# Second feed-forward part: six of eight weight pairs by seven products, three sum buffers, x added in the output, and low parts made two granules at a time

## The chip, the cores and the metric

The kernel runs on 1 core of one Trainium2 chip. The metric is the device time of one execution in microseconds (us), lower is better. Engines by their names in the profile: PE (TensorE, matrix products), DVE (VectorE), ACT (ScalarE), POOL (GpSimd) and SP (SyncE); the last two mainly start DMA transfers. Each engine runs its own instructions in the order written, and engines wait for each other by semaphores.

## What is computed

Two transformer-like blocks over 256 tokens of width 2048, all in fp32. The change lies in the last part of the second block, the feed-forward part with relu squared, called FFN 2 here:

```python
D_MODEL = 2048; SEQ = 256; D_FF_2 = 4 * D_MODEL
h2 = rms_norm(x, g_ff[l])
x = x + jnp.square(jax.nn.relu(h2 @ w_ff1[l])) @ w_ff2[l]
```

The first block has a feed-forward part of its own (FFN 1, gated by silu), which uses some of the same helper functions.

## The kernel before

**Numbers in two parts.** Each fp32 operand is split into a high part (fp32r, a copy by ACT) and a low part (the number minus its high part, by DVE). A product is three matmuls: high x high, low x high, high x low. Each matmul here has a stationary 128x128 and a moving 128x512 operand.

**Weights.** SP loads them by 1 MB into `raw`, a ring of four slots of two *granules* each; a granule is 2 chunks of 128 rows x 512 columns. ACT (`hi`) writes the high part into `w_hi`, DVE (`lo`) the low part into `w_lo`; both are rings of only 4 granules. `hi` of a granule waits in `gran_used` until PE has used the granule four before it; `lo` waits for `hi`; PE waits for both (`hi_ready`, `lo_ready`). The load into a raw slot waits for the `lo` of what was there.

**Turns.** FFN 2 handles 8192 hidden columns in turns of 1024 (`block2(at, i)`, i = 0 to 6). A turn has first 8 *units* 0 to 7: unit u is the pair of chunks 2u, 2u+1 of w_ff1 over 1024 columns (two granules). Then four *panels* 2 to 5 of w_ff2: 4 granules each (g = 0 to 3, written (panel, g)), 12 matmuls a granule, which multiply the hidden columns of the turn before and are 512 columns of the output each. The hidden columns made by turn i are thus used in turn i+1. The last turn has four more panels, 6 to 9.

**Units by seven products.** An *ordinary* unit is 8 block products, 24 matmuls. A unit *by products* takes 7 products (21 matmuls) as in Strassen's scheme in Winograd's form: it needs four sums of weight blocks (`sums_seven` on DVE: three instructions into `t_sum`), their high parts (`hi_sums`, ACT) and low parts (`lo_sums`, DVE: two instructions), the low parts of three blocks (`lo_blocks`, 128x1536) and four sums of token blocks, made once (`s_forms`, `first_forms`). Turn 0 has units 1, 3, 5, 7 by products (`SEVEN`), turns 1 to 6 units 0, 1, 3, 5, 7 (`FIVE`). There are two sum buffers. The sums of units 0 and 1 of the next turn are made while PE is in panel 5.

**Behind the units.** `recombine` (DVE) puts the products together into `hid` and `gates` (two rows of 512 columns). ACT takes relu times the token's factor (`relu_rows`) into another buffer, DVE multiplies the two (scalar_tensor_tensor), `flip` transposes in blocks (DVE), `move` on POOL finishes the transpose by 16 DMAs, and `hid_turn` makes the high part (ACT) and the low part (DVE) of the result, `low_hi` and `low_lo`, which panels 2 to 5 of the next turn read.

**Output.** PE accumulates a panel in one of two bank pairs in PSUM (q0 and q1, `pairs`), or `aux`. After panels 2 to 5 DVE adds it to x, which lies in SBUF (`xres`), by `add_x`, and counts `evac_done`; `bank_free` on PE waits for that before the pair's next use. At the end SP stores `xres` to the output.

**Order.** Each engine's order is written out by hand in its own `block2`. In DVE's, around panel 5: lo of panel 5 with `sums_seven(0)` in between, `lo_sums(0)`, `add_x(4)`, `sums_seven(1)`, `lo_blocks(0)`, `add_x(5)`, `lo_blocks(1)`, `lo_sums(1)`.

## Time and profile before

| | us |
|---|---|
| median of 3 runs (2574.84 to 2575.89) | 2574.9 |
| span of the profiled execution | 2573.7 |
| PE busy | 2567.3 (100%) |
| DVE busy | 2015.8 (78%) |
| ACT busy | 1451.4 (56%) |
| POOL busy | 536.5 (21%) |
| turn 0 of FFN 2 (1938.67 to 2023.08) | 84.41 |
| turn 2 of FFN 2 (2107.05 to 2191.02) | 83.97 |

The profiled execution is told by its span, from the first to the last instruction. Busy times of PE overlap between matmuls, since their ends are modelled, so the distance between two starts tells what a matmul takes. In the text *busy* says nothing of waits; what an engine waited for stands in square brackets behind a row of a timeline.

### The profile page before, as it was taken

How to read it: one execution, taken by the hardware profiler on the slowest of the kernel's cores; microseconds unless marked ns; L12 is line 12 of the kernel's file. 1: busy time of each engine (PE TensorE's matmuls, PEld its weight loads, DVE VectorE, ACT ScalarE, POOL GpSimd, SP SyncE). 2: the span in 40 equal slices, each digit the busy share in tenths (PEclk: the TensorE clock that was granted, in tenths of full speed). 3: DMA queues.
4: the chain of work that ended last, by engine and by line, in shares of the span. 5: the costliest groups of instructions: out<-in, count | busy, mean ns of one | idle time of the engine just before them, and what ended most of it. 6: DMA issues, size and time to landing. Idle time of an engine off the chain costs nothing.

```text
span 2573.7 us, 34186 instructions
## 1 busy us (share of the span) xinstructions
PE 2567.3 (100%) x11501; PEld 2134.4 (83%) x11501; DVE 2015.8 (78%) x2102; ACT 1451.4 (56%) x1615; POOL 536.5 (21%) x1034
## 2 busy tenths in 40 slices
...
GB/s 274 210 206 212 216 197 208 255 214 209 209 238 246 245 241 244 247 242 243 240 291 216 210 183 195 174 191 211 223 202 215 231 206 218 201 220 206 206 228 154
DMA packets 291153, 564.76 MB, mean 219 GB/s; under 512 B 28512, under 2 KB 41872, under 8 KB 290544
## 3 DMA queue, kind: packets, MB, share of 16 engines
...
q10 hardware_dynamic: 176, 0.07, 0.0%
...
## 4 chain that ended last, share of the span: by engine, by line
PE 97%; DVE 1%; DMA 1%; SPq 0%; DVEq 0%; ACT 0%; issue 0%; ACTq 0%
PE pair L2491 22%; PE pair L2486 22%; PE pair L2495 22%; PE pair L2776 8%; PE aux L2776 6%; PE aux L2761 3%; PE aux L2755 3%; PE aux L2758 3%; PE pair L2758 1%; PE pair L2755 1%; PE pair L2761 1%; PE aux L2653 0%; DMA raw<-in_w_ffn_down 0%; PE aux L2648 0%; PE pair L2573 0%; PE pair L2566 0%
## 5 line engine op out<-in xcount | busy, mean ns | idle before, releaser
L845 ACT ACTIVATE w_hi<-raw 128x1024 fp32r<-128x1024 f32 (+1 forms) x786 | 818.2, 1053 | 722.1 <-PE pair L2495 571.4
L1499 DVE TENSOR_TENSOR w_lo<-raw,w_hi 128x1024 fp32r<-128x1024 f32 (+1 forms) x788 | 937.7, 1214 | 342.1 <-ACT w_hi L845 323.2
L2486 PE MATMUL pair<-w_hi,lhs_hi 128*128 128x512 f32 x1568 | 422.6, 391 | 0.8 <-ACT lhs_hi L897 0.8
L2491 PE MATMUL pair<-w_hi,lhs_lo 128*128 128x512 f32 x1568 | 419.7, 389 | 0.6 <-DVE lhs_lo L1552 0.5
L2495 PE MATMUL pair<-w_lo,lhs_hi 128*128 128x512 f32 x1568 | 419.7, 389 | 0.0
L766 POOL DMA_DIRECT2D arena<-arena x528 | 262.4, 603 | 668.9 <-DVE arena L2003 291.0
L2491 PEld LDWEIGHTS pair<-w_hi,lhs_lo 128*128 128x128 f32 x1568 | 294.2, 188 | 63.0 <-DVE lhs_lo L1552 1.4
L2495 PEld LDWEIGHTS pair<-w_lo,lhs_hi 128*128 128x128 f32 x1568 | 294.0, 188 | 62.2 <-DVE w_lo L1499 1.0
L2486 PEld LDWEIGHTS pair<-w_hi,lhs_hi 128*128 128x128 f32 x1568 | 292.2, 188 | 60.6 <-ACT lhs_hi L897 1.2
L2486 PE MATMUL pair<-w_hi,low_hi 128*128 128x512 f32 (+1 forms) x992 | 263.4, 387 | 0.0
L2491 PE MATMUL pair<-w_hi,low_lo 128*128 128x512 f32 (+1 forms) x992 | 262.0, 386 | 0.0
L2495 PE MATMUL pair<-w_lo,low_hi 128*128 128x512 f32 (+1 forms) x992 | 261.7, 385 | 0.0
L2491 PEld LDWEIGHTS pair<-w_hi,low_lo 128*128 128x128 f32 x992 | 185.7, 188 | 36.3
L2495 PEld LDWEIGHTS pair<-w_lo,low_hi 128*128 128x128 f32 x992 | 185.5, 188 | 36.3
L2486 PEld LDWEIGHTS pair<-w_hi,low_hi 128*128 128x128 f32 x992 | 185.5, 188 | 36.0
L1180 ACT ACTIVATE w_hi<-raw 128x1536 fp32r<-128x1536 f32 x74 | 110.3, 1490 | 150.2 <-PE aux L2776 93.9
L777 POOL DMA_DIRECT2D arena<-arena x256 | 125.1, 497 | 251.9 <-DVE arena L1545 181.6
L2042 DVE TENSOR_TENSOR t_lo<-t_sum,t_hi 128x1024 fp32r<-128x1024 f32 x148 | 174.2, 1218 | 0.4 <-ACT t_hi L1189 0.2
L1189 ACT ACTIVATE t_hi<-t_sum 128x1024 fp32r<-128x1024 f32 x148 | 150.7, 1053 | 28.7 <-PE aux L2776 18.2
L2033 DVE TENSOR_TENSOR w_lo<-raw,w_hi 128x1536 fp32r<-128x1536 f32 x74 | 130.1, 1758 | 35.6 <-ACT w_hi L1180 21.0
L786 POOL DMA_DIRECT2D xres<-sums x36 | 46.8, 1314 | 437.8 <-ACT sums L1199 399.0
L2761 PE MATMUL aux<-w_lo,lhs_hi 128*128 128x512 f32 x372 | 124.6, 389 | 0.0
(366 smaller groups left out, 3244.1 us busy)
## 6 DMA issues: line engine op xcount, KB each, us to landing
raw<-in_w_ff SPq DMA_DIRECT2D x128, 1024.0 KB, 5.2
raw<-in_w_in SPq DMA_DIRECT2D x118, 1024.0 KB, 5.3
raw<-in_w_ffn_down SPq DMA_DIRECT2D x44, 1024.0 KB, 5.1
raw<-in_w_ffn_gate SPq DMA_DIRECT2D x80, 512.0 KB, 6.6
raw<-in_w_ffn_up SPq DMA_DIRECT2D x80, 512.0 KB, 7.5
raw<-in_w_out SPq DMA_DIRECT2D x32, 1024.0 KB, 5.7
...
xres<-sums POOLq DMA_DIRECT2D x36, 512.0 KB, 9.8
```

Source lines behind the costliest of these rows:

```text
L766: pool.dma_start(dst[f * 32:(f + 1) * 32, a], src[a * 32:(a + 1) * 32, f]).then_inc(moved, 16)
L777: pool.dma_start(turn_t[n % 2][f * 32:(f + 1) * 32, a], turn_x[n % 2][a * 32:(a + 1) * 32, f]).then_inc(row_moved[n % 2], 16)
L845: nc.scalar.activation(w_hi[:, at.slot(p, k), :, 0:width], raw[:, at.raw_slot(p, k), 2 * h:2 * h + 2, 0:width], ACT.Copy).then_inc(hi_read ...
L1189: nc.scalar.activation(t_high[:, 2 * h:2 * h + 2], t[:, 2 * h:2 * h + 2], ACT.Copy).then_inc(t_hi_ready, 1)
L1499: v.tensor_tensor(w_lo[:, at.slot(p, k), :, 0:n], raw[:, at.raw_slot(p, k), 2 * h:2 * h + 2, 0:n], w_hi[:, at.slot(p, k), :, 0:n].bitcast( ...
L2033: v.tensor_tensor(two_slots(w_lo, at, p, k)[:, 1:4], raw[:, at.raw_slot(p, k), 1:4], two_slots(w_hi, at, p, k)[:, 1:4].bitcast(F32), ALU.s ...
L2042: v.tensor_tensor(t_low[:, 2 * h:2 * h + 2], t[:, 2 * h:2 * h + 2], t_high[:, 2 * h:2 * h + 2].bitcast(F32), ALU.subtract).then_inc(t_lo_r ...
L2486: nc.tensor.matmul(ps[:, t, 0:n], hi_t[:, ch, tok], w_hi[:, s, c, 0:n], start=start and k == 0 and c == 0, stop=False)
L2491: nc.tensor.matmul(ps[:, t, 0:n], lo_t[:, ch, tok], w_hi[:, s, c, 0:n], start=False, stop=False)
L2495: mm = nc.tensor.matmul(ps[:, t, 0:n], hi_t[:, ch, tok], w_lo[:, s, c, 0:n], start=False, stop=stop and 2 * k + c == kch - 1)
L2761: mm = nc.tensor.matmul(bank[t, w], lhs_hi[:, ch, tok], w_lo[:, s, w, :], start=False, stop=u == 6 and c == 1 and (t, w) == (1, 0))
L2776: mm = nc.tensor.matmul(bank, s, t, start=fresh and first and a, stop=last and z)
```

## The change

- In turns 1 to 6 units 0, 1, 3, 4, 6, 7 go by products (`SIX`), in turn 0 units 1, 3, 4, 6, 7 (`FIVE`). Units 2 and 5 are ordinary.
- There are three sum buffers (`ring`). The third lies over `xres`, whose first three quarters are stored to the output before FFN 2 (SP, `x_stored`).
- Panels 2, 3 and 4 are no longer added to x on DVE: ACT copies them (`copy_part`) into `gates` or `hid`, and POOL adds them to the output by an accumulating DMA (`add_part`). Panel 5 is still added by `add_x`.
- Relu squared is made on ACT alone, in place (`relu_squares`: two Relu, one Square); DVE's multiplications go.
- `lo_two` makes the low parts of two granules in one instruction, 128x2048, and counts both when it is done.
- The orders of DVE, ACT, POOL and PE in a turn are rewritten. In `seven` the product with block B21 comes third, then the two with T1 and T3, then T2 (before: T2 third); this holds for FFN 1 too.

The diff, cut to its core:

```diff
-FIVE = (0, 1, 3, 5, 7)
+FIVE = (1, 3, 4, 6, 7)
+SIX = (0, 1, 3, 4, 6, 7)
+MAIN = {SEVEN: SEVEN, FIVE: FIVE[1:], SIX: FIVE[1:]}
...
+    ring = [(over_x(xres), [t_hi2[:], t_lo2[:, :, 2 * N:3 * N]], over_x(t_lo2)),
+            (halves(t_sum[0]), halves(t_hi), halves(t_lo[0])),
+            (halves(t_sum[1]), halves(t_hi1), halves(t_lo[1]))]
...
+            sp.wait_ge(evac_done, At("out2").panel(2) + 1 + EVAC_CREDIT)
+            sp.dma_start(token_rows(out[0])[:, :, 0:3 * N], xres[:, :, 0:3 * N]).then_inc(x_stored, 16)
...
+            def add_part(j, i):
+                pool.wait_ge(sums_copied, i * 3 + (COPIES1 + j + 1))
+                pool.sem_inc(moving, 1)
+                pool.dma_start(token_rows(out[0])[:, :, j * N:(j + 1) * N], hid if j == 1 else gates,
+                               accum_op=ALU.add).then_inc(parts_added[j % 2], 16)
+            move(NB1 + T_FF2)
+            pool.wait_ge(x_stored, 16)
+            with pool.Fori(0, TURNS2 - 1) as i:
+                for n in range(2):
+                    move(i * 2 + (NB1 + T_FF2 + 1 + n))
+                for j in range(3):
+                    add_part(j, i)
...
+            def relu_squares(rows):
                 for t in range(TOK):
-                    nc.scalar.activation(dst[:, t, :], src[t], ACT.Relu, scale=x_inv[:, t:t + 1])
+                    nc.scalar.activation(rows[:, t, :], rows[:, t, :], ACT.Relu, scale=x_inv[:, t:t + 1])
+                act.drain()
+                nc.scalar.activation(rows, rows, ACT.Square)
                 act.drain().then_inc(act_ready, 1)
-            def block2(at, i, last=False, five=True):
+            def copy_part(at, p, j, i):
+                panel_done(at, p)
+                if p < 4:
+                    act.wait_ge(flipped, i * 2 + (NB1 + T_FF2 + 3 + j))
+                if j == 2 or not isinstance(i, int) or i > 0:
+                    act.wait_ge(parts_added[j % 2], i * 16 if j == 1 else i * 32 + 8 * j)
+                nc.scalar.activation(hid if j == 1 else gates, pairs[at.pair(p)][:], ACT.Copy
+                                     ).then_inc(sums_copied, 1)
...
+            def block2(at, i, last=False, units=SIX):
                 n = i + TURNS1
                 b = i * 2 + NB1
...
+                act.wait_ge(gran_used, at.gran(0) + SPLIT)
+                if units == FIVE:
+                    hi_sums(3, n, units)
+                hid_turn(b, 0, T_FF2 - 1)
+                hi_ordinary(at, 2, None)
+                hi_seven(at, 3, None)
+                hi_sums(4, n, units)
+                hi_seven(at, 4, None)
+                hi_ordinary(at, 5, None)
+                hi_sums(6, n, units)
+                hi_seven(at, 6, None)
+                hi_sums(7, n, units)
+                hi_seven(at, 7, None)
                 hi(at, 2, 0, 2)
                 act.wait_ge(products, n * 3 + 1)
                 nc.scalar.activation(first_product, aux[:, 0, :], ACT.Copy).then_inc(product_copied, 1)
+                hid_turn(b + 1, 4, T_FF2 - 1)
                 hi(at, 2, 2, 4)
                 act.wait_ge(gates_ready, n + 1)
...
+                relu_squares(gates)
                 hi(at, 3, 0, 1)
...
+                relu_squares(hid)
                 hi(at, 3, 1, 4)
+                copy_part(at, 2, 0, i)
+                if units == FIVE:
+                    act.wait_ge(s_sums_ready, 4)
+                    nc.scalar.activation(zero_hi[:], zero_sum[:], ACT.Copy).then_inc(s_hi_ready, 1)
                 hi(at, 4, 0, 4)
...
+                copy_part(at, 3, 1, i)
                 hi(at, 5, 0, 4)
...
                 else:
                     nxt = At("ffn2", i + 1)
...
+                    hi_sums(0, n + 1, SIX)
+                    copy_part(at, 4, 2, i)
+                    hi_seven(nxt, 0, None)
+                    hi_sums(1, n + 1, SIX)
+                    hi_seven(nxt, 1, None)
+                    hi_sums(3, n + 1, SIX)
...
+            def lo_two(at, p, k):
+                dve.wait_ge(hi_ready, at.gran(p, k) + 2)
+                v.tensor_tensor(two_slots(w_lo, at, p, k), raw[:, at.raw_slot(p, k)],
+                                two_slots(w_hi, at, p, k).bitcast(F32), ALU.subtract).then_inc(lo_ready, 2)
...
+            def block2(at, i, last=False, units=SIX):
                 n = i + TURNS1
                 b = i * 2 + NB1
...
+                if units == FIVE:
+                    sums_seven(at, 3, n, units)
+                    lo_sums(3, n, units)
+                    dve.wait_ge(x_stored, 16)
                 hid_turn(b)
...
+                lo_two(at, *unit(2))
+                lo_blocks(at, 3)
+                sums_seven(at, 4, n, units)
+                lo_sums(4, n, units)
+                lo_blocks(at, 4)
+                lo_two(at, *unit(5))
+                sums_seven(at, 6, n, units)
+                sums_seven(at, 7, n, units)
+                lo_sums(6, n, units)
+                lo_blocks(at, 6)
+                lo_sums(7, n, units)
+                lo_blocks(at, 7)
+                lo_two(at, 2, 0)
+                if units == SIX:
+                    dve.wait_ge(parts_added[0], i * 32)
+                    dve.wait_ge(parts_added[1], i * 16)
+                recombine(at, n, 3, units, lambda: hid_turn(b + 1, 4))
+                lo_two(at, 2, 2)
                 dve.wait_ge(act_ready, b + 3)
...
+                flip(b + (2 + T_FF2), by_chunk(gates), n_split=1)
+                lo_two(at, 3, 0)
+                lo_two(at, 3, 2)
+                if units == FIVE:
+                    pair_forms(0, zero_pair, zero_sum)
+                lo_two(at, 4, 0)
+                lo_two(at, 4, 2)
                 dve.wait_ge(act_ready, b + 4)
...
                 flip(b + (3 + T_FF2), by_chunk(hid), n_split=1)
...
+                if units == FIVE:
+                    dve.wait_ge(s_hi_ready, 4)
+                    v.tensor_tensor(zero_lo[:], zero_sum[:], zero_hi[:].bitcast(F32), ALU.subtract)
                     dve.drain().then_inc(s_ready, 1)
...
                 else:
                     nxt = At("ffn2", i + 1)
...
+                    lo_two(at, 5, 0)
+                    sums_seven(nxt, 0, n + 1, SIX)
+                    lo_two(at, 5, 2)
+                    lo_sums(0, n + 1, SIX)
+                    sums_seven(nxt, 1, n + 1, SIX)
                     lo_blocks(nxt, 0)
+                    lo_sums(1, n + 1, SIX)
+                    sums_seven(nxt, 3, n + 1, SIX)
                     add_x(at, 5, 3 * N)
                     lo_blocks(nxt, 1)
...
+                    lo_sums(3, n + 1, SIX)
...
+                product(aux[:, 3, :], form(S4), block_of(B21), fresh).then_inc(gran_used, 2)
+                if last:
+                    second().then_inc(products, 1)
+                if u == 0:
+                    bank_free(at, 1)
+                pe.wait_ge(t_lo_ready, sevens(i, u, units) * 2 + 1)
+                product(q1[:, 0, :], form(S1), sum_of(T1), True)
+                mm = product(q1[:, 1, :], form(S3), sum_of(T3), True)
                 if last:
                     mm.then_inc(products, 1)
-                product(aux[:, 3, :], form(S4), block_of(B21), five).then_inc(gran_used, 2)
-                if five and u == 0:
-                    bank_free(at, 1)
-                product(q1[:, 1, :], form(S1), sum_of(T1), True)
-                mm = product(q1[:, 0, :], form(S3), sum_of(T3), True)
-                if last:
-                    mm.then_inc(products, 1)
-                product(aux[:, 2, :], tokens(1, c + 1), sum_of(T4), five).then_inc(t_used, 1)
+                else:
+                    second()
+                product(aux[:, 2, :], tokens(1, c + 1), sum_of(T4), fresh).then_inc(t_used, 1)
...
+            def block2(at, i, units=SIX):
+                n = i + TURNS1
+                if units == FIVE:
+                    bank_free(at, 0)
+                    ordinary(at, 0, units)
                     bank_free(at, 1)
...
+                    pe.wait_ge(s_ready, 3)
                 else:
...
+                    pe.wait_ge(sums_copied, i * 3 + COPIES1)
+                    pe.wait_ge(s_ready, 4)
+                    bank_free(at, 0)
+                    seven(at, 0, n, units)
                 for u in range(1, 8):
...
+                    if u in units:
+                        seven(at, u, n, units)
                     else:
...
+                        ordinary(at, u, units)
+                bank_free(at, 2)
+                for g in range(2):
+                    pe.wait_ge(moved_taken, i * 2 + (NB1 + T_FF2 + 1 + g))
+                    gemm(at, 2, low, groups=[g])
+                gemm(at, 3, low)
+                for j in range(2, 4):
+                    gemm(at, 2 + j, low, free=copied(i * 3 + (COPIES1 + j - 1)))
```

Of the lines that the diff takes away from the two `block2` of ACT and DVE and from that of PE none is shown; they stand in the kernel before.

**DVE, from panel 5 of turn 0 into turn 1.** `t_sum_78`, `t_sum_79` and (after) `xres` are the sum buffers, `w_lo` 128x1536 is `lo_blocks`, `xres<-xres,pair` is `add_x(5)`, `w_lo` 128x1024 is `lo` and 128x2048 is `lo_two`. Before:

```order
L1499 TENSOR_TENSOR w_lo<-raw,w_hi 128x1024 [waits hi_ready] x2
L2042 TENSOR_TENSOR t_lo_76<-t_sum_78,t_hi 128x1024 [waits t_hi_ready] x2
L1937 TENSOR_TENSOR xres<-xres,pair 128x2x512 [waits gran_used]
L2021 TENSOR_TENSOR t_sum_79<-raw 128x1024 [waits t_used,raw_loaded1]
L2024 TENSOR_TENSOR t_sum_79<-raw,t_sum_79 128x512
L2026 TENSOR_TENSOR t_sum_79<-raw,t_sum_79 128x512
L2033 TENSOR_TENSOR w_lo<-raw,w_hi 128x1536 [waits hi_ready]
L1937 TENSOR_TENSOR xres<-xres,pair 128x2x512 [waits gran_used]
L2033 TENSOR_TENSOR w_lo<-raw,w_hi 128x1536 [waits hi_ready]
L2042 TENSOR_TENSOR t_lo_77<-t_sum_79,t_hi_80 128x1024 [waits t_hi_ready] x2
```

The same place after, from the sums of unit 1 on:

```order
L2102 TENSOR_TENSOR t_sum_78<-raw 128x1024 [waits t_used,raw_loaded1]
L2105 TENSOR_TENSOR t_sum_78<-raw,t_sum_78 128x512
L2107 TENSOR_TENSOR t_sum_78<-raw,t_sum_78 128x512
L2114 TENSOR_TENSOR w_lo<-raw,w_hi 128x1536 [waits hi_ready]
L2123 TENSOR_TENSOR t_lo_76<-t_sum_78,t_hi 128x1024 [waits t_hi_ready] x2
L2102 TENSOR_TENSOR t_sum_79<-raw 128x1024 [waits t_used,raw_loaded3]
L2105 TENSOR_TENSOR t_sum_79<-raw,t_sum_79 128x512
L2107 TENSOR_TENSOR t_sum_79<-raw,t_sum_79 128x512
L2012 TENSOR_TENSOR xres<-xres,pair 128x2x512 [waits gran_used]
L2114 TENSOR_TENSOR w_lo<-raw,w_hi 128x1536 [waits hi_ready]
L2123 TENSOR_TENSOR t_lo_77<-t_sum_79,t_hi_80 128x1024 [waits t_hi_ready] x2
```

The low parts of unit 1's sums and the sums of unit 3 (`raw_loaded3`) now stand ahead of `add_x(5)` and of unit 1's `lo_blocks`; the `add_x(4)` behind the first `lo_sums` is gone.

**ACT, in turn 1 between panels 2 and 3.** `w_hi<-raw` is `hi`, `arena<-arena` works on `gates` and `hid`. Before:

```order
L1437 ACTIVATE arena<-arena,small 128x512 [waits gates_ready]
L1437 ACTIVATE arena<-arena,small 128x512
L843 REGISTER_ALU [waits raw_loaded2]
L845 ACTIVATE w_hi<-raw 128x1024 [waits gran_used]
L1459 REGISTER_ALU
L1437 ACTIVATE arena<-arena,small 128x512 [waits hid_ready]
L1437 ACTIVATE arena<-arena,small 128x512
```

After:

```order
L1488 ACTIVATE arena<-arena,small 128x512 [waits gates_ready]
L1488 ACTIVATE arena<-arena,small 128x512
L1490 ACTIVATE arena<-arena 128x1024
L892 REGISTER_ALU [waits raw_loaded2]
L894 ACTIVATE w_hi<-raw 128x1024 [waits gran_used]
L1488 ACTIVATE arena<-arena,small 128x512 x2
L1490 ACTIVATE arena<-arena 128x1024
```

Each pair of Relu now has a Square of 128x1024 behind it, ahead of the next `w_hi` of panel 3: granule (3,0) behind the first, (3,1) behind the second.

## Rows read from the trace of the kernel before

Rows of a timeline: start us, duration us, engine, line, operation, output<-inputs, shapes, how many in a row, and in brackets what ended an idle time before it. Of the window table: from:to, length, then busy us (and instructions) of PE, PEld, DVE, ACT, POOL, then the granted clock of TensorE, the DMA share and GB/s. Of the page's groups: busy us, mean ns of one | idle before, releaser; of its DMA issues: KB each, us to landing.

**Rows 1.** The page: span, busy time of each engine, the chain by engine.

```profile
span 2573.7 us, 34186 instructions
...
PE 2567.3 (100%) x11501; PEld 2134.4 (83%) x11501; DVE 2015.8 (78%) x2102; ACT 1451.4 (56%) x1615; POOL 536.5 (21%) x1034
...
PE 97%; DVE 1%; DMA 1%; SPq 0%; DVEq 0%; ACT 0%; issue 0%; ACTq 0%
```

**Rows 2.** Window table, the turn i = 2 of FFN 2 (columns below).

```profile
2107.05:2191.02 83.97, 83.97 (x370) 69.18 (x369) 75.61 (x70) 45.38 (x44) 15.62 (x32) 1.00 0.66 212
```

**Rows 3.** Timeline of PE where a turn of FFN 2 starts.

```profile
2106.02 1.07 PE L2495 MATMUL pair<-w_lo,low_hi 128*128 128x512 f32 x4
2107.05 0.50 PE L2776 MATMUL aux<-w_hi,lhs_hi 128*128 128x512 f32 x1
2107.39 0.40 PE L2776 MATMUL aux<-w_hi,lhs_lo 128*128 128x512 f32 x1
...
2112.02 0.39 PE L2776 MATMUL aux<-w_hi,lhs_hi 128*128 128x512 f32 x1
...
2116.78 0.39 PE L2755 MATMUL aux<-w_hi,lhs_hi 128*128 128x512 f32 x1
```

**Rows 4.** Timeline of DVE, panel 5 and the start of the next turn.

```profile
2098.48 2.35 DVE L2042 TENSOR_TENSOR t_lo<-t_sum,t_hi 128x1024 fp32r<-128x1024 f32 x2
2100.75 1.21 DVE L1937 TENSOR_TENSOR xres<-xres,pair 128x1024 f32<-128x1024 f32 x1
2102.15 1.23 DVE L2021 TENSOR_TENSOR t_sum<-raw 128x1024 f32<-128x1024 f32 x1 [0.19 <-issue]
...
2105.24 1.76 DVE L2033 TENSOR_TENSOR w_lo<-raw,w_hi 128x1536 fp32r<-128x1536 f32 x1 [0.27 <-issue]
2107.12 1.22 DVE L1937 TENSOR_TENSOR xres<-xres,pair 128x1024 f32<-128x1024 f32 x1
2108.77 1.76 DVE L2033 TENSOR_TENSOR w_lo<-raw,w_hi 128x1536 fp32r<-128x1536 f32 x1 [0.43 <-ACT w_hi L1180]
2110.45 2.35 DVE L2042 TENSOR_TENSOR t_lo<-t_sum,t_hi 128x1024 fp32r<-128x1024 f32 x2
...
2122.00 1.22 DVE L1996 TENSOR_TENSOR low_lo<-arena,low_hi 128x1024 fp32r<-128x1024 f32 x1
...
2172.99 1.25 DVE L2003 STREAM_TRANSPOSE arena<-arena 128x1024 f32<-128x1024 f32 x1 [0.20 <-issue]
```

**Rows 5.** Timeline of ACT: the w_hi of granule (5,3).

```profile
2096.25 1.06 ACT L845 ACTIVATE w_hi<-raw 128x1024 fp32r<-128x1024 f32 x1 [1.66 <-PE pair L2495]
```

**Rows 6.** Timeline of DVE ahead of turn 0: a subtraction of 2048 columns.

```profile
1928.37 2.28 DVE L2381 TENSOR_TENSOR s_lo<-s_sum,s_hi 128x2048 fp32r<-128x2048 f32 x1
```

**Rows 7.** Timeline of PE: first product of unit 7.

```profile
2142.62 0.39 PE L2776 MATMUL aux<-w_hi,lhs_hi 128*128 128x512 f32 x1
```

**Rows 8.** Timeline of DVE: the recombination's second step, and w_lo behind it.

```profile
2146.90 1.23 DVE L2059 TENSOR_TENSOR arena<-pair,arena 128x1024 f32<-128x1024 f32 x1 [0.40 <-PE pair L2776]
...
2151.34 2.36 DVE L1499 TENSOR_TENSOR w_lo<-raw,w_hi 128x1024 fp32r<-128x1024 f32 x2 [0.19 <-issue]
```

**Rows 9.** Timeline of ACT: relu of gates, and the w_hi behind it.

```profile
2151.21 1.34 ACT L1437 ACTIVATE arena<-arena,small 128x512 f32<-128x512 f32 x2 [3.66 <-DVEq L2071]
2152.72 1.06 ACT L845 ACTIVATE w_hi<-raw 128x1024 fp32r<-128x1024 f32 x1 [0.17 <-issue]
```

**Rows 10.** Timeline of DVE in turn 0: relu_square of the first stage's panel 1.

```profile
1942.22 1.40 DVE L2369 SCALAR_TENSOR_TENSOR arena<-pair,small,arena 128x512 f32<-128x512 f32 x2
```

**Rows 11.** The page: one group of instructions, and two groups of DMA issues.

```profile
L786 POOL DMA_DIRECT2D xres<-sums x36 | 46.8, 1314 | 437.8 <-ACT sums L1199 399.0
...
raw<-in_w_ff SPq DMA_DIRECT2D x128, 1024.0 KB, 5.2
...
xres<-sums POOLq DMA_DIRECT2D x36, 512.0 KB, 9.8
```

**Rows 12.** Timeline of PE: the longest wait between two matmuls of weights.

```profile
1325.82 1.20 PE L2486 MATMUL pair<-w_hi,lhs_hi 128*128 128x512 f32 x4 [0.77 <-ACT lhs_hi L897]
```

307 lines of the change are left out of this document (140 added, 167 removed).

## The prediction, made before the changed kernel ran

> **What bounds the kernel now.** I read the page first: TensorE (PE) is busy 2567.3 of 2573.7 us and the chain that ended last lies 97% on it [rows 1]. Then the window table: one turn of the second feed-forward part takes 83.97 us, TensorE is busy in all of it, VectorE (DVE) in 75.61, ScalarE (ACT) in 45.38, and the granted clock is 1.00 [rows 2]. Two questions follow: what does one matmul cost, and how much room does VectorE have at the place where it is late?
>
> The matmul: unit 1 (21 products) runs from 2112.02 to 2116.78, so 226.7 ns each [rows 3]. A unit by products takes 4.76 us, an ordinary unit (24) 5.44, a granule of a w_ff2 panel (12) 2.72, a panel 10.88. A turn has 5 x 21 + 3 x 24 + 192 = 369 matmuls, 83.65 us; it takes 0.32 more. That 0.32 stands at its start: the last granule's third row starts at 2106.02 and ends its issue at 2106.93, unit 0 starts at 2107.05, its second product comes 0.34 later where 0.23 is usual, and unit 0 takes 4.97 [rows 3]. Its releaser is lo_blocks(0) on VectorE, 2105.24 + 1.76 = 2107.00 [rows 4]. So VectorE is already exactly as late as it may be at the turn's start, though it is busy only 90% of the turn. It cannot use the idle tenth, which lies in the panels, since there each w_lo waits for a w_hi whose slot TensorE has just left: the w_hi for granule (5,3) starts at 2096.25, 0.2 after panel 5 began [rows 5].
>
> **The change, part by part.** I count time from the end of panel 5 (0 = 2106.93 in the trace). After the change the units want to start at 0, 4.76, 9.52 (ordinary), 14.96, 19.72, 24.48 (ordinary), 29.92 (unit 6), 34.68 (unit 7), 39.44 (panel 2).
>
> *Matmuls.* One more pair by products in each of 7 turns: 21 matmuls less, 21 x 0.2267 = **-4.8 us**, all on the path. The 0.32 at the start of turns 1 to 6 is contained in what follows, so it is taken off: **-2.0**.
>
> *VectorE's prices.* From start to start [rows 4]: the two instructions of lo_sums 2.27, add_x 1.40, the three of sums_seven with what follows their drain 3.09, lo_blocks 1.68; hid_turn is 1.22 with 0.08 of overlap, 1.14. A 128x2048 subtraction took 2.28 [rows 6], so lo_two is 2.21 where two of lo are 2.27: making low parts two at a time saves 0.07 to 0.14 a pair, and costs that the first granule's low part comes out only with the second's.
>
> *VectorE's total.* Per turn: plus one unit by products (2.27 + 3.09 + 1.68 = 7.04), minus one ordinary unit (2.27), minus three add_x (4.2), minus the four scalar_tensor_tensor of relu (two took 1.40 [rows 10], so 2.8), minus some 10 x 0.1 of merging. That is about -3: the total fits the turn. But the place counts, not the total. The three add_x and the relu products were in the panels, where VectorE idled; the new sums are between panel 5 and unit 7.
>
> *Where that chain starts.* hi(4,3) is ready 1.3 after panel 3 ends [rows 5], at -20.5; lo_two(4,2) until -18.3; flip of hid (1.25 [rows 4]) until -16.9. The new copy_part(3,1) on ScalarE waits for that flip, and hi(5,0..3) are queued behind it: copy 1.06 (a bound from the 1024-wide ACTIVATE [rows 5]), hi(5,0) and hi(5,1) until -13.7. lo_two(5,0) until -11.4, sums_seven(0) until -8.5. Without that copy it would be hi(5,3) that decides: -9.6.
>
> *What the chain must do by unit 6.* lo_two(5,2), two more lo_two (units 2, 5): 3 x 2.21 = 6.63. lo_sums of 0, 1, 3, 4, 6: 5 x 2.27 = 11.35. sums_seven of 1, 3, 4, 6, 7: 5 x 3.09 = 15.45. lo_blocks of 0, 1, 3, 4, 6: 5 x 1.68 = 8.40. hid_turn 1.14, add_x 1.40. Sum 44.4, and 0.5 of waits for ScalarE's halves, since lo_sums(4) now follows sums_seven(4) directly. -8.5 + 44.9 = 36.4, against 29.92 wanted: **unit 6 starts 6.5 us late**. lo_blocks(7) at 40.4 is then in time for unit 7 (41.1). On the way TensorE waits earlier: lo_blocks(0) at 0.7; then q1's bank, because add_x(5) now stands behind sums_seven(3) and ends at -8.5 + 16.0 = 7.5, while unit 0 asks for it after nine products. These waits are parts of the 6.5, not added to it. In the kernel before the same stretch had one unit fewer, two sums fewer behind this point, and add_x(5) and lo_blocks(1) came at 2107.12 and 2108.77 [rows 4]. Six starts of a turn: 6 x 6.5 = **+39.0**.
>
> *Panels 2 and 3.* Counted from the start s of unit 7 (2142.62 [rows 7]). VectorE's recombination takes from 2146.90 to 2151.34, 4.4 [rows 8]; it now starts 1.1 later, since hid_turn stands between its first and second step: gates ready at s + 9.8 instead of 8.7. lo_two(2,2) comes at s + 12.1, wanted at s + 12.0: 0.1. On ScalarE relu took 1.51 to the next instruction [rows 9] and now has a Square behind it, 1.06 more: relu_squares(gates) until s + 12.4, hi(3,0) 13.4, relu_squares(hid) 16.1, hi(3,1) 17.2. Only then can lo_two(3,0) run, until s + 19.5, wanted at s + 4.76 + 10.88 + 1.81 = 17.5. TensorE waits **2.0**. Before, lo(3,0) needed only hi(3,0) of 2152.72, 5.5 before panel 3 [rows 7, 9]. 7 turns x 2.1 = **+14.7**.
>
> *Turn 0.* pair_forms and one_lo put some 2.7 ahead of relu_square, whose end (1942.22 + 1.4 before [rows 10]) releases q1 for unit 1: 1946.3 instead of wanted 1944.1, +2.2. Then flip, sums_seven(3), lo_sums(3) and hid_turn stand ahead of unit 2's low parts: 1957.3 against 1952.9, +4.4. Unit 4 +0.8, unit 6 +2.1 by the same pitches. **+9.5**.
>
> *Restarts.* After each wait the next matmul but one came 0.11 late [rows 3]; the walk has about five waits a turn: 7 x 5 x 0.11 = **+3.9**.
>
> *Adding x in the output.* Three more issues on POOL a turn at 1.3 each and a landing of 9.8, as xres<-sums has them in FFN 1 [rows 11]; gates must be free again for copy_part(4,2): issued at about s + 22, landed at s + 33, wanted at s + 41, hidden by 8. The x store (1.5 MB on SP's queue ahead of the first wide loads, three output blocks' worth) is taken as hidden by the ring of four raw slots; if not, it delays them by at most its own landing, 1.5 x 5.2 = 8, once [rows 11]. At the end the last accumulation starts about 1 after panel 8's end and lands within what the tail of 96 short matmuls takes (13 us): 0 to 3, I take **+0.5**. FFN 1, whose product order changes too, has its sums ready earlier than asked: 0.
>
> *The clock.* TensorE waited 0.77 at 1325.82 [rows 12] and the granted clock stayed 1.00; a wait of nearly 5, as in unit 0, stands nowhere in this trace. The Trainium skill, "TensorE: Matmul & The Clock Gate", section "HAM oscillation — how this bites in real kernels", says that waits inside a loop can put the clock back to its lower level each time round; no row here shows that. I take 0 and make it a rival.
>
> **Sum:** -4.8 - 2.0 + 39.0 + 14.7 + 9.5 + 3.9 + 0.5 = +60.8 on the execution of 2573.7. The median of the runs is 1.2 above it: 2573.7 + 60.8 + 1.2 = **2636 us**, 2.4% slower.
>
> **Rivals.**
> *VectorE keeps ahead (faster).* If the chain started some 7 us earlier or were that much shorter, none of the waits would be there: 2573.7 - 6.8 + 0.5 + 1.2 = 2569. For it: VectorE's total falls, and sums_seven needs no slot of w_hi. Against it: the written order puts lo_two(5,2), tied to the end of panel 4, ahead of everything. It decides at whether lo_blocks(6) is done 29.9 after panel 5's end.
> *The chain is late, but by less.* Without copy_part's hold-up (-9.6) and without the wait in panel 3, 5.4 a turn start and some 7 in turn 0: 2573.7 - 6.8 + 32.4 + 7 + 3 + 1.2 = 2610. With the dearest pieces hidden too (only the work that unit 7 itself needs, 2.2 late a turn): 2585.
> *The clock falls.* TensorE's 12 products behind the wait in unit 0 at half rate cost 12 x 0.227 = 2.7 a turn more, 19 in all: 2655. By the skill's rule named above this would be the case; by the row at 1325.82 the clock outlasts at least short waits.
>
> **Chances.** The forecast 0.62 (its own range, 1.5 a turn either way with some for turn 0: 2615 to 2654). Less late 0.14, clock 0.12, faster 0.09, no difference by cancellation 0.03. 80% range: 2590 to 2658, which leaves out the faster case, the lowest of the second and the highest of the clock's. A measurement of this kernel can tell about 0.2%; the faster case (-0.24%) is over it. Faster 0.09, same 0.03, slower 0.88.
>
> **What the profile after would show.** If I am right: windows of about 92 us a turn with 366 matmuls; TensorE waiting in unit 0 for xres<-xres,pair and w_lo, in unit 6 for the 128x1536 w_lo, at panel 3's first third row for the 128x2048 w_lo behind ScalarE's w_hi; VectorE without a gap from lo_two(5,2) to unit 7; turn 0's wait at unit 2. Wrong: TensorE without waits at the turn's start (the start of the chain misread), waits in panel 4 or 5 or for raw (loads or accumulations matter after all), or a granted clock under 1.00.

## The result and the profile after

The changed kernel takes **2654.3 us** (median of 4 runs, 2653.3 to 2655.2) beside 2575.2 for the kernel before (2574.8 to 2575.9): a ratio of 1.0307, 95% interval 1.0292 to 1.0321. It is 79 us slower; the forecast was 61 us slower (2636, range 2590 to 2658). The sign, the place and most of the amount were right, and 18 us were missing.

The page of after, answering [rows 1]: TensorE falls from 100% busy to 98%, and its share of the chain that ended last from 97% to 81%. What came in is VectorE (8%, and 4% as its queue's semaphores), ScalarE (3%) and 3% in which no wait shows (issue).

```profile
span 2652.0 us, 34342 instructions
...
PE 2588.0 (98%) x11480; PEld 2139.0 (81%) x11480; DVE 1998.9 (75%) x2012; ACT 1494.1 (56%) x1661; POOL 566.3 (21%) x1058
...
PE 81%; DVE 8%; DVEq 4%; ACT 3%; issue 3%; DMA 1%; SPq 1%; ACTq 0%
```

TensorE's busy time rose by 21 us, though it does 21 matmuls fewer. The window of one turn, answering [rows 2], says why: 95.56 us where 83.97 stood, 87.48 of them busy, and a granted clock of 0.96 where it was 1.00. VectorE's work fell (73.14 us, 75.61 before), as the prediction said, and did not help.

```profile
2225.28:2320.84 95.56, 87.48 (x366) 70.35 (x366) 73.14 (x58) 51.25 (x51) 19.38 (x35) 0.96 0.67 203
```

TensorE's timeline at the start of that turn, answering [rows 3], has a wait at the start, nine products, a wait of over 4 us for q1's bank, and then products 0.43 us apart, which is the 1.2 GHz level of the clock, against 0.23 at 2.4 GHz:

```profile
2225.28 0.50 PE L2869 MATMUL aux<-w_hi,lhs_hi 128*128 128x512 f32 x1 [0.67 <-DVE w_lo L2114]
...
2227.24 0.40 PE L2869 MATMUL aux<-w_lo,zero_hi 128*128 128x512 f32 x1
2231.83 0.79 PE L2869 MATMUL pair<-t_hi,zero_hi 128*128 128x512 f32 x1 [4.19 <-DVEq L2013]
2232.42 0.63 PE L2869 MATMUL pair<-t_hi,zero_lo 128*128 128x512 f32 x1
2232.84 0.63 PE L2869 MATMUL pair<-t_lo,zero_hi 128*128 128x512 f32 x1
...
2237.91 0.39 PE L2869 MATMUL aux<-w_lo,lhs_hi 128*128 128x512 f32 x1
```

Later in the same turn unit 6 and panel 3 start late:

```profile
2264.45 0.50 PE L2869 MATMUL aux<-w_hi,lhs_hi 128*128 128x512 f32 x1 [1.54 <-DVE w_lo L2114]
...
2289.01 1.21 PE L2588 MATMUL pair<-w_lo,low_hi 128*128 128x512 f32 x4 [1.44 <-DVE w_lo L2086]
```

VectorE's timeline of that turn, answering [rows 4]: lo_two(5,2) at 2215.91, lo_blocks(0) at 2223.46, add_x(5) at 2230.41, then lo_blocks(3), lo_blocks(4) and lo_two(5) for unit 5, each behind a gap that a w_hi of ScalarE ended, and lo_blocks(6) at 2262.64.

```profile
2215.91 2.29 DVE L2086 TENSOR_TENSOR w_lo<-raw,w_hi 128x2048 fp32r<-128x2048 f32 x1 [0.27 <-issue]
...
2223.46 1.76 DVE L2114 TENSOR_TENSOR w_lo<-raw,w_hi 128x1536 fp32r<-128x1536 f32 x1 [0.27 <-issue]
...
2230.41 1.22 DVE L2012 TENSOR_TENSOR xres<-xres,pair 128x1024 f32<-128x1024 f32 x1 [0.20 <-issue]
...
2241.38 1.76 DVE L2114 TENSOR_TENSOR w_lo<-raw,w_hi 128x1536 fp32r<-128x1536 f32 x1 [2.13 <-ACT w_hi L1229]
...
2249.63 1.76 DVE L2114 TENSOR_TENSOR w_lo<-raw,w_hi 128x1536 fp32r<-128x1536 f32 x1 [1.21 <-ACT w_hi L1229]
2252.13 2.29 DVE L2086 TENSOR_TENSOR w_lo<-raw,w_hi 128x2048 fp32r<-128x2048 f32 x1 [0.74 <-ACT w_hi L894]
...
2262.64 1.75 DVE L2114 TENSOR_TENSOR w_lo<-raw,w_hi 128x1536 fp32r<-128x1536 f32 x1
```

TensorE's waits between 1940 and 2660, by line and what they waited for (us in total, times, the longest):

```profile
PE pair L2869 <- DVEq L2013: 24.9, 6, 4.2
```

The others are those for lo_blocks (13.6 us), for lo_two in the panels (12.0), and 6.0 in five single waits, 4.4 of them in turn 0. Where below a wait is given as the distance of two starts above the usual 0.227, it is 0.17 longer than these figures: 4.36 for 4.19.

### The profile page after: what moved, and what is told of

Read it like the earlier page. It is cut to its first block, busy times and chain, and to the rows that moved or that the text cites. A ratio compares the mean times of both kernels' runs of the same rounds, so it can differ in the third digit from the quotient of the medians.

```text
span 2652.0 us, 34342 instructions
## 1 busy us (share of the span) xinstructions
PE 2588.0 (98%) x11480; PEld 2139.0 (81%) x11480; DVE 1998.9 (75%) x2012; ACT 1494.1 (56%) x1661; POOL 566.3 (21%) x1058
## 4 chain that ended last, share of the span: by engine, by line
PE 81%; DVE 8%; DVEq 4%; ACT 3%; issue 3%; DMA 1%; SPq 1%; ACTq 0%
PE pair L2588 18%; PE pair L2579 18%; PE pair L2584 18%; PE pair L2869 7%; PE aux L2869 5%; DVEq L2104 3%; PE aux L2848 2%; PE aux L2854 2%; PE aux L2851 2%; ACT w_hi L894 2%; DVE t_sum L2102 1%; PE pair L2848 1%; PE pair L2851 1%; PE pair L2854 1%; DVE w_lo L2086 1%
## 5 line engine op out<-in xcount | busy, mean ns | idle before, releaser
L894 ACT ACTIVATE w_hi<-raw 128x1024 fp32r<-128x1024 f32 (+1 forms) x772 | 799.8, 1052 | 632.4 <-PE pair L2588 524.6
L1574 DVE TENSOR_TENSOR w_lo<-raw,w_hi 128x1024 fp32r<-128x1024 f32 (+1 forms) x630 | 749.8, 1213 | 311.2 <-ACT w_hi L894 297.8
L2086 DVE TENSOR_TENSOR w_lo<-raw,w_hi 128x2048 fp32r<-128x2048 f32 x72 | 164.4, 2291 | 106.7 <-ACT w_hi L894 102.8
L2584 PEld LDWEIGHTS pair<-w_hi,low_lo 128*128 128x128 f32 x992 | 185.7, 188 | 36.4
L1238 ACT ACTIVATE t_hi<-t_sum 128x1024 fp32r<-128x1024 f32 x136 | 138.8, 1054 | 103.1 <-DVEq L2104 55.3
L1229 ACT ACTIVATE w_hi<-raw 128x1536 fp32r<-128x1536 f32 x81 | 120.5, 1487 | 122.6 <-PE aux L2869 61.8
L2114 DVE TENSOR_TENSOR w_lo<-raw,w_hi 128x1536 fp32r<-128x1536 f32 x81 | 142.3, 1757 | 46.8 <-ACT w_hi L1229 35.7
L2123 DVE TENSOR_TENSOR t_lo<-t_sum,t_hi 128x1024 fp32r<-128x1024 f32 x136 | 160.2, 1220 | 1.8 <-issue 1.0
```

What stands on the lines that cost most here:

```text
L894: nc.scalar.activation(w_hi[:, at.slot(p, k), :, 0:width], raw[:, at.raw_slot(p, k), 2 * h:2 * h + 2, 0:width], ACT.Copy).then_inc(hi_read ...
L1238: nc.scalar.activation(t_high[h], t[h], ACT.Copy).then_inc(t_hi_ready, 1)
L1574: v.tensor_tensor(w_lo[:, at.slot(p, k), :, 0:n], raw[:, at.raw_slot(p, k), 2 * h:2 * h + 2, 0:n], w_hi[:, at.slot(p, k), :, 0:n].bitcast( ...
L2086: v.tensor_tensor(two_slots(w_lo, at, p, k), raw[:, at.raw_slot(p, k)], two_slots(w_hi, at, p, k).bitcast(F32), ALU.subtract).then_inc(lo_ ...
L2114: v.tensor_tensor(two_slots(w_lo, at, p, k)[:, 1:4], raw[:, at.raw_slot(p, k), 1:4], two_slots(w_hi, at, p, k)[:, 1:4].bitcast(F32), ALU.s ...
L2123: v.tensor_tensor(t_low[h], t[h], t_high[h].bitcast(F32), ALU.subtract).then_inc(t_lo_ready, 1)
```

## The experiments

Two theories stood. Mine: VectorE's chain from panel 5 to unit 6 is too long and stands in an unlucky order, and the clock adds something once waits are long. Rivals: the waits stand each for themselves; the sixth pair as such is what costs; or the clock alone is the missing 18 us.

**a_addx: only add_x(5) moved ahead.** It was written behind lo_sums(1) and sums_seven(3).

```
                     lo_blocks(nxt, 0)
+                    add_x(at, 5, 3 * N)
                     lo_sums(1, n + 1, SIX)
                     sums_seven(nxt, 3, n + 1, SIX)
-                    add_x(at, 5, 3 * N)
                     lo_blocks(nxt, 1)
```

> The changed kernel with one instruction of VectorE moved: add_x(5) stands ahead of lo_sums(1) and sums_seven(3) instead of behind them; nothing else. Theory (order of VectorE, and a clock that falls behind the long wait in unit 0): the wait of 4.4 us inside unit 0 goes, since add_x(5) ends about 2 us after panel 5 instead of 7.5; lo_blocks(1) keeps its place in time, so TensorE now waits about 3.3 us at the start of unit 1. If only a wait of over 4 us brings the granted clock down, unit 0 and 1 run at 227 ns a matmul and some 3 us a turn are saved: 2654 - 18 = 2636 us, clock 1.000. Rival 1 (a wait of 3.3 us does it too): time as before, 2652 to 2656, clock 0.993. Rival 2 (the chain on VectorE alone sets the turn, the clock costs nothing): 2650 to 2656 with clock 1.000.

Measured 2647.0 us, ratio 1.0279 (1.0262 to 1.0296). This lies between the theory (2636) and the two rivals (2650 and more). The wait for q1 is gone, and in its place TensorE waits 3.46 at unit 1 for lo_blocks(1). Unit 6 waits 1.71 as before. The wait grew shorter and the clock fell all the same, behind five of the six:

```profile
2229.09 0.79 PE L2869 MATMUL aux<-w_hi,lhs_hi 128*128 128x512 f32 x1 [3.30 <-DVE w_lo L2114]
2229.69 0.63 PE L2869 MATMUL aux<-w_hi,lhs_lo 128*128 128x512 f32 x1
```

So my split at 4 us was wrong: 41 products at 0.43 behind waits of 3.3 to 3.5, where after has 61.

The wait that did not lower it, in turn 2, is as long (3.46). That gives two turns of one run that differ in the clock alone. The turn from 2128.85 to 2220.67 lasts 91.82 us, and the gaps in which VectorE waits for a w_hi up to unit 5 come to 0.46; the next, to 2315.09, has 12 slow products, lasts 94.42, and the gaps come to 3.03. Both wait 3.46 at unit 1 and 1.71 at unit 6. First the turn with the upper clock (the first TensorE product, the one gap), then the three gaps of the other:

```profile
2137.28 0.50 PE L2869 MATMUL aux<-w_hi,lhs_hi 128*128 128x512 f32 x1 [3.30 <-DVE w_lo L2114]
2137.62 0.40 PE L2869 MATMUL aux<-w_hi,lhs_lo 128*128 128x512 f32 x1
...
2152.04 2.29 DVE L2086 TENSOR_TENSOR w_lo<-raw,w_hi 128x2048 fp32r<-128x2048 f32 x1 [0.46 <-ACT w_hi L894]
```

```profile
2234.99 1.76 DVE L2114 TENSOR_TENSOR w_lo<-raw,w_hi 128x1536 fp32r<-128x1536 f32 x1 [0.34 <-ACT w_hi L1229]
...
2243.96 1.76 DVE L2114 TENSOR_TENSOR w_lo<-raw,w_hi 128x1536 fp32r<-128x1536 f32 x1 [1.94 <-ACT w_hi L1229]
2246.47 2.29 DVE L2086 TENSOR_TENSOR w_lo<-raw,w_hi 128x2048 fp32r<-128x2048 f32 x1 [0.75 <-ACT w_hi L894]
```

The slow products (12 x 0.20, and 0.25 more at the restart) make VectorE late by the 2.6 us that they take, so they cost their full length, although VectorE's chain is what TensorE waits for at unit 6.

**b_relu: w_hi of (3,1) ahead of relu_squares(hid) on ScalarE.**

```
-                hi(at, 3, 0, 1)
+                hi(at, 3, 0, 2)
...
-                hi(at, 3, 1, 4)
+                hi(at, 3, 2, 4)
```

> The changed kernel with ScalarE's w_hi of granule (3,1) ahead of relu_squares(hid) instead of behind it. Theory: the wait of 1.6 us in panel 3, which ends with lo_two(3,0), hangs on that w_hi alone; it goes in all 7 turns with its restart of 0.11: 2654 - 12 = 2642 us, the wait at unit 0, 1, 6 unchanged. Rival (VectorE or the flip behind it is as late): a wait of over 1 us stays in panel 3 or comes in panel 4, over 2650 us.

Measured 2638.6 us, ratio 1.0246 (1.0229 to 1.0263). The waits for lo_two in the panels fell from 12.0 to 1.7 us and no other wait moved: the term "panels 2 and 3" of the sum is confirmed as to its mechanism, and the trace shows its size. The 15.7 us that came back are more than the 12 expected, since the clock moved too: behind the same six waits of 4.2 to 4.4 in unit 0 there are 33 slow products where after has 61, 5.6 us less. Why they are fewer is open.

**c_lo1: low parts one granule at a time again.** lo_two becomes two of the old instructions.

```
-                dve.wait_ge(hi_ready, at.gran(p, k) + 2)
-                v.tensor_tensor(two_slots(w_lo, at, p, k), raw[:, at.raw_slot(p, k)], ...).then_inc(lo_ready, 2)
+                lo(at, p, k, k + 2)
```

> The changed kernel with lo_two made as two instructions of 128x1024, each counted when done; all else as changed. Theory: the wait in panel 3 (1.6 us, 7 times) goes, since the low part of (3,0) no longer waits for the w_hi of (3,1), the 0.4 in panel 2 too; VectorE's chain from panel 5 to unit 6 grows by 3 x 0.06. Together about -13: 2641 us. Rival (merging two granules is what saves VectorE's time, and its being late by a granule hurts nowhere): slower than 2654, by up to 8.

Measured 2617.2 us, ratio 1.0163 (1.0146 to 1.0180): 37 us come back, three times what I expected. Per turn it is 89.13 for 95.57, and the waits say where the 6.4 come from: no wait in panels 2 and 3 (2.2 with the restarts), none at the turn's start (0.9), 3.25 for q1 instead of 4.36 with a short restart (1.4), 0.94 at unit 6 instead of 1.71 (0.8), 7 slow products instead of 12 (1.0). VectorE's timeline tells why. Counted from the end of panel 5, the low part of (5,2) now begins at -10.6 and not -8.5: each pair of granules in panels 4 and 5 no longer waits for its second w_hi, so flip, copy_part and the sums of pair 0 all come earlier. And of the gaps of 2.13, 1.21 and 0.74 ahead of unit 5's low parts, 0.88 and 1.18 are left:

```profile
2312.51 1.76 DVE L2112 TENSOR_TENSOR w_lo<-raw,w_hi 128x1536 fp32r<-128x1536 f32 x1 [0.88 <-ACT w_hi L1229]
...
2320.72 1.76 DVE L2112 TENSOR_TENSOR w_lo<-raw,w_hi 128x1536 fp32r<-128x1536 f32 x1 [1.18 <-ACT w_hi L1229]
```

I had priced lo_two by its duration, 0.07 saved; what it costs is the wait for the second granule, at the head of a chain.

**f_early2: the sums of pairs 0 and 1 each one step earlier,** ahead of lo_two(5,0) and lo_two(5,2).

> The changed kernel with sums_seven(0) ahead of lo_two(5,0) and sums_seven(1) ahead of lo_two(5,2) on VectorE; nothing else. Theory (the wait at a turn's start is the length of VectorE's chain behind lo_two(5,2), and that chain now has one sum of 3.1 us less and starts at the same time): add_x(5) ends 3.1 us earlier and more, the wait in unit 0 falls from 4.4 to about 1.5, the 0.8 at the turn's start and the 1.7 at unit 6 shrink or go, and the clock stays at its upper level (no matmuls at 427 ns). Some 6 to 7 us a turn less: 2654 - 6 x 6.5 = 2615 us. Rival (the clock falls after any wait of 2 us too): some 12 matmuls at 427 ns a turn stay, 2630 us. Rival (ScalarE or the loads set the start): change under 1 us a turn, 2648 us or more.

Measured 2640.0 us, ratio 1.0249 (1.0232 to 1.0266): between the rivals of 2630 and 2648, and far from the theory's 2615. The wait at the start is gone, the one for q1 is 3.6 to 5 (2.6 in the last turn), the clock fell behind all six, and unit 6 is as late as ever. On VectorE sums_seven(0) waited 0.82 and sums_seven(3) 0.52 for their loads: so these two sums can't be made any earlier at these places.

**d_five: five pairs by products (0, 1, 3, 4, 7) in turns 1 to 6,** unit 6 made ordinary; order otherwise as changed.

> The changed kernel with five pairs by seven products in turns 1 to 6 (0, 1, 3, 4, 7; unit 6 ordinary), as many as the kernel before has; the third sum buffer, the output path and the orders stay. Theory (the order at the turn's start, not the number of products): VectorE has 4.8 us less to do ahead of unit 7, the wait at unit 6 (1.7 us) goes, but the waits in unit 0 and the slow clock behind them stay, and 3 matmuls more cost 0.7: 2654 - 6 x 1.1 = 2647 us. Rival (six pairs by products are simply too much for VectorE): all waits in the units go, 2654 - 6 x 12 + 4 = about 2586 us.

Measured 2648.9 us, ratio 1.0284 (1.0267 to 1.0301). The wait at unit 6 is gone, those in unit 0 (4.35) and panel 3 (1.64) are untouched. With the number of pairs that the kernel before has, 73 of the 79 us remain. So it isn't the sixth pair. That it is where the work stands is for the orders below to show.

**i_one and i_two: the kernel before, with more work on VectorE.** The subtraction of lo_blocks(0) is made once, and twice, more than needed at each turn's start.

```
-                    lo_blocks(nxt, 0)
+                    lo_blocks(nxt, 0, 1)      (2 in i_two)
```

> The kernel before, and its subtraction for the low parts of pair 0's three blocks (1.75 us on VectorE) made once more than needed at each of the six turn starts; nothing else differs. All of VectorE's chain of that turn comes 1.75 us later and TensorE waits 1.8 us instead of 0.1 at the turn's start, and nowhere else, since every later step is as late as TensorE itself. Theory (a wait of up to 2 us leaves the clock alone): matmuls after it 227 ns apart, six times 1.75 us = 10.5 us, 2585.5 us. Rival (each wait longer than 1 us at a turn's start lowers the clock for 12 matmuls, 2.6 us): 2601 us.

> As the run before, with the subtraction made twice more than needed: one wait of about 3.6 us at each of the six turn starts. Without any effect on the clock that is six times 3.5 = 21 us, 2596 us. Theory (a wait of over 3 us lowers the granted clock from 2.4 to 1.2 GHz for some 12 to 15 matmuls behind it, 0.2 us each, and the restart costs 0.36 instead of 0.11): 2.65 to 3.25 us more a turn, 2612 to 2616 us, with matmuls 427 ns apart in the trace. Rival (the slow stretches of the changed kernel come of several waits close together, not of one long one): 2596 us, spacing 227 ns throughout.

Measured 2587.8 us (ratio 1.0051, 1.0034 to 1.0068) and 2607.0 us (1.0125, 1.0108 to 1.0142). The six waits of 1.9 us in i_one leave the clock at 1.00, and no product behind them is slow. In i_two they are 3.7 to 3.9 us, and the clock falls behind five of the six:

```profile
2203.24 0.79 PE L2780 MATMUL aux<-w_hi,lhs_hi 128*128 128x512 f32 x1 [3.58 <-DVE w_lo L2037]
2203.83 0.63 PE L2780 MATMUL aux<-w_hi,lhs_lo 128*128 128x512 f32 x1
2204.26 0.63 PE L2780 MATMUL aux<-w_lo,lhs_hi 128*128 128x512 f32 x1
```

i_two is 19.3 us above i_one. Six waits longer by 1.8 give 11, 38 products at 0.43 give 7.6, and restarts come on top. One long wait alone is thus enough, but it doesn't cost the same each time: 0, 5, 13, 7, 7 and 6 slow products. I had expected 12 to 15 behind each; the result lies between theory and rival because of that.

**g_best2: a first attempt at a better kernel.** Sums early as in f_early2, low parts singly, add_x(5) and lo_blocks(1) ahead, in most units lo_blocks ahead of lo_sums, relu behind the w_hi of panel 3, and four pairs (1, 3, 6, 7) in turn 0. It changes all of these at once, so no single order can be priced from it.

> The changed kernel with all three findings in its orders: sums_seven(0) and (1) made in VectorE's idle time in panel 4 and 5, add_x(5) and lo_blocks(1) ahead of sums_seven(3), each lo_blocks ahead of its lo_sums where both are waited for, low parts one granule at a time, relu behind the w_hi of panel 3, hid_turn ahead of the recombination; in turn 0 four pairs by products (1, 3, 6, 7). Six pairs by products in turns 1 to 6, the output path and the three sum buffers stay. Theory (the loss of the change lay in the order, not in what it does): waits of TensorE in a turn under 1 us, clock 1.000, 366 matmuls a turn at 227 ns: 2575 - 18 x 0.227 - 2 + up to 5 = 2569 to 2575 us. Rival (VectorE cannot do six pairs in time in any order: 46 us of work between panel 5 and unit 7 against 44 there): 2 to 3 us of waits a turn, 2585 to 2592 us. Rival (the accumulating transfers or ScalarE's copies cost by themselves): waits in panels 4 and 5 or for raw, over 2580 us.

Measured 2623.1 us, ratio 1.0182 (1.0165 to 1.0199), far from the 2569 to 2575 expected. Its waits moved from VectorE to ScalarE: unit 7 waits for w_hi, because the high parts of the sums, which come late, stood ahead of it in ScalarE's queue (20.1 us in 8 waits), and panel 2 waits 2.0 for the first step of recombining. The wait at unit 7 (2.9 us) lowers the clock too, in three of six turns:

```profile
2343.02 0.50 PE L2880 MATMUL aux<-w_hi,lhs_hi 128*128 128x512 f32 x1 [2.71 <-ACT w_hi L896]
2343.36 0.40 PE L2880 MATMUL aux<-w_hi,lhs_lo 128*128 128x512 f32 x1
2343.59 0.41 PE L2880 MATMUL aux<-w_lo,lhs_hi 128*128 128x512 f32 x1
2343.82 0.61 PE L2880 MATMUL pair<-w_hi,lhs_hi 128*128 128x512 f32 x1
```

**k_early: c_lo1 with add_x(5) and lo_blocks(1) ahead of sums_seven(3).**

```
                     lo_sums(1, n + 1, SIX)
+                    add_x(at, 5, 3 * N)
+                    lo_blocks(nxt, 1)
                     sums_seven(nxt, 3, n + 1, SIX)
-                    add_x(at, 5, 3 * N)
-                    lo_blocks(nxt, 1)
```

> The changed kernel with low parts made singly (as in c_lo1, 2617 us), and x added to panel 5 and the low parts of pair 1's blocks both moved ahead of the sums of pair 3. Theory (VectorE's work up to unit 6 is one full chain, so its length sets the turn and not its order): the waits inside unit 0 and at unit 1 (3.25 us a turn) go, the wait at unit 6 grows from 0.9 to 4.2 to 5 us, turns of 88 to 90 us, 2610 to 2620 us. Rival (the waits stand for themselves): six times 3.3 us and the slow clock, 1.4 us, go: 2617 - 28 = 2589 us.

Measured 2603.1 us, ratio 1.0109 (1.0092 to 1.0126), between the two expectations. The waits did move, as the chain theory says, though by less than it says (unit 6 was to wait 4.2 to 5): 3.25 at q1 became 0.25, and 1.3 at unit 4 and 1.9 at unit 6 stand where 0.94 was. But turns are 87.07, 2.06 shorter than c_lo1's, and 2.06 is what c_lo1's two gaps ahead of w_hi add up to (0.88 + 1.18). They are gone:

```profile
2282.04 2.36 DVE L1574 TENSOR_TENSOR w_lo<-raw,w_hi 128x1024 fp32r<-128x1024 f32 x2 [0.20 <-issue]
...
2305.46 1.75 DVE L2112 TENSOR_TENSOR w_lo<-raw,w_hi 128x1536 fp32r<-128x1536 f32 x1
...
2324.79 1.75 DVE L2112 TENSOR_TENSOR w_lo<-raw,w_hi 128x1536 fp32r<-128x1536 f32 x1
```

From 2282.04 to 2326.54 the chain takes 44.5 us, the 44.4 of the prediction's own addition. In the changed kernel it takes 48.5 (2215.91 to 2264.39), in c_lo1 46.6. The difference is the gaps, each time: 4.1, 2.1, 0. The gaps are TensorE's own lateness coming back. The w_hi of pair 3 needs the slots of pair 1, and in the changed kernel ScalarE stands 5.62 us until TensorE frees them; in k_early it does not wait (first row after, second k_early):

```profile
2239.79 1.49 ACT L1229 ACTIVATE w_hi<-raw 128x1536 fp32r<-128x1536 f32 x1 [5.62 <-PE aux L2869]
```

```profile
2303.45 1.47 ACT L1229 ACTIVATE w_hi<-raw 128x1536 fp32r<-128x1536 f32 x1
```

**h_best, n_best and n_five: how near to the kernel before can an order come?** h_best is g_best2 with the high parts of units 6 and 7 ahead of those of their sums, recombining's first step directly behind unit 7's low parts, and lo_blocks(0) ahead of lo_sums(1). n_best takes k_early's order of the turn's start instead. n_five is n_best with pairs 0, 1, 3, 4 and 7 alone.

> As g_best2 (sums of the next turn's pairs 0 and 1 made early, low parts singly, four pairs by products in turn 0), with three orders mended: ScalarE makes the high parts of units 6 and 7 before those of their sums, VectorE makes the first step of recombining directly behind the sums' low parts of unit 7, and the low parts of pair 1's sums come behind those of pair 0's blocks. Theory (g_best2's waits came of these three): waits at unit 6 (0.6), unit 7 (2.9), panel 2 (2.0) and at the turn's start (0.7) shrink to 1 us a turn together, turns of 84 to 85 us, 2575 to 2585 us. Rival (VectorE's chain of a turn with six pairs is too long in any order, and the waits only move): turns of 88 us, 2605 us or more.

> h_best (2594.8 us, turns of 84.7 to 86.8) with k_early's order of the turn's start put back (low parts of panel 5's first two granules ahead of the sums of pair 0, sums of pair 1 behind the low parts of pair 0's sums), and low parts singly in the last turn's panels too. In h_best the sums of pair 0 waited for their load, the waits in unit 0 and at the turn's start were 1.4 and 0.3 us a turn, where k_early has 0.25 and none. Theory: these go, and unit 7's 0.7 stays: six times 1.4 us less, 2586 us (2582 to 2590). Rival (what is removed at the start comes back at units 4 to 7, since the work of VectorE between them is the same): 2592 to 2597 us.

> n_best with five pairs by seven products in turns 1 to 6 (0, 1, 3, 4, 7; unit 6 ordinary) in place of six: three matmuls a turn more, 0.68 us, six times 4.1 us, and 4.6 us a turn less work for VectorE. Theory (in n_best the waits behind unit 4 are those of VectorE's chain, 1.0 us a turn): they go, turns of 84.2 us, 1.9 us less in all than n_best, that is the same within what can be measured. Rival A (n_best's waits at units 4 to 7 are larger, so the sixth pair costs more than it brings): 5 us or more below n_best, down to the kernel before's 2575. Rival B (the waits are not of VectorE's chain): 4 us above n_best.

Measured 2594.8 us (1.0075, 1.0058 to 1.0092), 2596.6 (1.0082, 1.0065 to 1.0099) and 2598.0 (1.0084, 1.0067 to 1.0100). h_best takes back 59 of the 79 us, by several moves at once; it lies between its two expectations. Its turns are 84.7 to 86.8 and seven of its products are slow. Putting k_early's start into it brought nothing: n_best waits 1.2 to 1.4 for q1 in all six turns, where h_best waits 1.0 to 1.4 in five, and 0.7 to 1.0 at the start of five turns, where h_best mostly waits 0.3. So that expectation failed. The rival's time came out, but not its mechanism: the waits at the start never went, and the 0.7 at unit 7 is the same in both. Five pairs are as good as six: the 0.7 wait at unit 7 goes and 0.68 us of matmuls comes. None of the three is faster than the kernel before. What holds n_best's turn start back is, by the trace, the flip of hid, which waits for the moves of the flip before it:

```profile
2252.24 1.25 DVE L2085 STREAM_TRANSPOSE arena<-arena 128x1024 f32<-128x1024 f32 x1
...
2267.48 1.25 DVE L2085 STREAM_TRANSPOSE arena<-arena 128x1024 f32<-128x1024 f32 x1 [2.02 <-DMA arena<-arena]
```

k_early's second flip has no such wait, with 16.5 us between its two flips. That this is what is left was read from the trace and not tested.

## Why the prediction came out as it did

Each term beside what the trace of after shows, as distances of TensorE's products above 0.227 us:

| term | predicted | measured |
|---|---|---|
| 21 matmuls fewer | -4.8 | -4.8 (a turn has 366 in the window) |
| waits at start, q1 and unit 6, turns 1 to 6 | +39.0 | +41.2 |
| panels 2 and 3, seven turns | +14.7 | +14.4 |
| turn 0 up to unit 7 | +9.5 | +7.0 |
| restarts | +3.9 | +5.4 |
| clock (slow products: 61 in turns 1 to 6, 6 in turn 0) | 0 | +13.4 |

With -2.0 for the old waits that makes 75 of the 78 us between the two spans. The other 3 lie in small distances, which I didn't sort, and at the end, which has 0.5 in the prediction. Of the 5.4 of restarts 1.5 are the clock's as well: six products behind waits were followed 0.36 late and not 0.11.

**Right.** The views led to the place: [rows 2] with its 75.61 of 83.97 looked like room, and [rows 4] showed that there was none where it counted. The chain starts at -8.5 (measured 2215.91, panel 5's last product ends its issue at 2224.45) and holds 44.4 us of work. The waits in unit 0, unit 6 and panel 3 stand where the walk put them, with the releasers that it named. The loads and the accumulation into the output stayed hidden: no wait of TensorE names them. Panel 3 waits 1.6 and not 2.0, since panel 2 is late by 0.4 itself; the two together are 2.0, beside 2.1 in the sum.

**The step that failed** is "I take 0" for the clock. The row it was weighed against, 0.77 of waiting at 1325.82 [rows 12], says nothing on a wait of 4.2, and no row of before could. The granted clock fell to the lower level behind each of the six waits in unit 0, for 61 products in all. By the rule of the Trainium skill, "TensorE: Matmul & The Clock Gate", section "HAM oscillation — how this bites in real kernels", waits inside a loop put the clock back each time round. That the trace of after now shows (0.96 in every steady turn), and i_two shows it of one wait alone; but behind waits of 3.1 to 3.7 us it was not each time round (a_addx's second, c_lo1's first and i_two's first left the clock where it was). I had priced that rival at 19 us, for 84 products in seven turns; 13.4 came, from 67 products at 0.20 more. The rival's total, 2655, lies within 1 us of the measured 2654.3, and that is chance: 1.5 more in restarts and 3 of small distances made up for it, and the waits of the forecast came out 2.2 higher at the units and 2.5 lower in turn 0. Behind it stands a second error: I gave the rule a chance of 0.12 as one of several exclusive cases, though my own forecast held such a wait, of nearly 5 us, in six turns. A case that follows from the forecast isn't a rival to it.

**A second step was too smooth:** "VectorE without a gap from lo_two(5,2) to unit 7", with 0.5 for ScalarE. There are gaps of 4.1 us, unit 6 starts at 39.9 and not at 36.4. The walk held TensorE on its wanted times while it let VectorE fall behind, and so had w_hi's slots free too early. The waits in unit 0 and the slow clock delay the slots, the slots delay w_hi, and w_hi delays the chain that TensorE waits for. Pair 3's w_hi needs a slot that unit 1's third product frees, and that product stands behind the wait for q1 and behind the 12 slow ones. The two turns of a_addx show the clock's share: 12 slow products there bring 2.6 us of gaps. By that some 2.6 of the 4.1 are the clock's and the rest the wait's own (an estimate carried over from a_addx to after). Since TensorE's waits at the start, the slow products and the restarts all lie inside the 10 us by which unit 6 is late, the clock's 13.4 and the gaps' 3.6 a turn (4.1 less the 0.5 that the prediction allowed) are two views of one amount and don't add. Between c_lo1 and k_early too, the turn differs by the gaps, 2.06, and TensorE's side shows the same amount as 1.4 of slow products and 0.7 of waits.

**By luck:** turn 0 was priced 2.5 too high (at unit 2 above all: 2.1 in place of 4.4), and its wait at unit 1 (2.5 us) also lowered the clock, for 1.2 us that no term held.

What stays open: which of the parts that were never tried alone (three sum buffers, the sum in the output) costs the last 20 us of h_best, if either does and not the order that is left; and why a wait of one length lowers the clock once and not another time.
